# A fifth expert buffer made out of the dense weight buffers, in a two-layer attention and mixture-of-experts kernel on one core

## The reference

```python
for l in range(DEPTH):                       # DEPTH = 2
    sh1, sc1, g1, sh2, sc2, g2 = adaln_params(cond, w_ada[l], b_ada[l])
    ... = mixer_inputs(modulate(x, sh1, sc1), w_in[l], ...)     # two token mixers
    y = merge_branches(o_na, o_mla, gate_na, gate_mla, *out_w)
    x = layer_norm(DEEPNORM_ALPHA * x + g1 * y, ln1_g[l], ln1_b[l])
    y = hierarchical_moe(modulate(x, sh2, sc2), *moe_w)
    x = layer_norm(DEEPNORM_ALPHA * x + g2 * y, ln2_g[l], ln2_b[l])

def hierarchical_moe(h, ...):                # 32 experts, each token goes to 2
    ...
    hid = silu(einsum('bsd,edf->bsef', h, w_gate)) * einsum('bsd,edf->bsef', h, w_up)
    hid = hid * combine[..., None]
    return einsum('bsef,efd->bsd', hid, w_down)
```

## Time and profile before

| What | Value |
|---|---|
| median of 3 runs | 1138.49 us |
| the profiled execution | 1141.46 us |
| its span in the profile | 1139.3 us |
| TensorE busy | 971.6 us (85%) |
| VectorE, ScalarE busy | 318.4 us, 188.4 us |
| read from HBM | 329.38 MB |
| layer 0: first expert matmul, last scatter ends | 350.9 us, 578.0 us |
| layer 1: the same | 893.3 us, 1121.0 us |

### The profile page before, as it was taken

How to read it: one execution, slowest core, us unless ns; L and a number is a source line. 1 busy time by engine, 2 the same in 40 slices (tenths; PEclk the granted TensorE clock), 3 DMA queues, 4 the chain that set the end, 5 groups by cost and what they waited for, 6 DMA issues and landing times.

```text
span 1139.3 us, 15627 instructions
## 1 busy us (share of the span) xinstructions
PE 971.6 (85%) x6804; PEld 597.2 (52%) x6804; DVE 318.4 (28%) x630; ACT 188.4 (17%) x387; POOL 0.2 (0%) x4
## 2 busy tenths in 40 slices
PE   4399999989848998989829999998984899898993
PEld 1288767777644434333217786677874543433331
DVE  1203322222372212111171142232237221211215
ACT  0001311400012211111110122150001121111111
POOL 0000000000000000000000000000000000000000
PEclk7599999999958999999968999999995899999997
DMA  9656544477884999999954674446594499999990
GB/s 359 230 221 242 210 156 186 151 291 270 359 360 168 428 429 428 429 428 427 427 175 152 246 254 146 175 159 229 199 392 205 158 430 427 427 429 429 429 393 39
DMA packets 43227, 332.98 MB, mean 292 GB/s; under 512 B 5528, under 2 KB 7928, under 8 KB 13968
## 3 DMA queue, kind: packets, MB, share of 16 engines
q1 hardware_dynamic: 33552, 308.82, 67.0%
q10 hardware_dynamic: 9600, 23.07, 6.1%
HBM read 329.38 MB, written 2.49 MB: 291 GB/s over the span
## 4 chain that ended last, share of the span: by engine, by line
PE 73%; DMA 14%; DVE 7%; issue 3%; ACT 1%; SPq 0%; ACTq 0%; DVEq 0%
PE ps L671 15%; PE ps L487 10%; PE ps L684 8%; DMA expert_gate_up<-in_w_gu 7%; PE ps L511 5%; PE ps L602 5%; PE ps L612 4%; PE ps L423 4%; DMA expert_down<-in_w_dn 3%; PE ps L649 3%; PE ps L536 3%; PE ps L437 3%; PE ps L523 2%; PE ps L694 2%; PE ps L568 2%
## 5 line engine op out<-in xcount | busy, mean ns | idle before, releaser
L671 PE MATMUL ps<-expert_gate_up,gatheredT 128*32 128x512 f32 x2048 | 229.1, 600 | 16.6 <-DMA expert_gate_up<-in_w_gu 16.0
L671 PEld LDWEIGHTS ps<-expert_gate_up,gatheredT 128*32 128x32 f32 x2048 | 71.0, 111 | 164.3 <-issue 164.3
L684 PE MATMUL ps<-expert_down,hiddenT 128*32 128x512 f32 x1024 | 115.2, 595 | 9.3 <-issue 5.0
L487 PE MATMUL ps<-hT,dense 128*128 128x256 f32 x512 | 114.2, 381 | 0.0
L487 PEld LDWEIGHTS ps<-hT,dense 128*128 128x128 f32 x512 | 96.1, 190 | 16.0 <-issue 3.6
L1308 DVE TENSOR_TENSOR hidden<-hidden,ps 128x256 f32<-128x256 f32 x32 | 13.5, 421 | 234.0 <-ACT hidden L929 234.0
L684 PEld LDWEIGHTS ps<-expert_down,hiddenT 128*32 128x32 f32 x1024 | 32.2, 109 | 80.2 <-issue 50.6
L1318 DVE SCALAR_TENSOR_TENSOR y_lo<-ps,slot_weight,y_hi 128x512 fp32r<-128x512 f32 x64 | 48.0, 750 | 93.2 <-ACT y_hi L941 93.2
L437 PE MATMUL ps<-const,h_tokens 128*128 128x128 f32 x64 | 15.0, 426 | 68.0 <-DVE h_tokens L1024 68.0
L423 PE MATMUL ps<-dense,cond 128*32 128x256 f32 x768 | 57.2, 421 | 16.2 <-ACT cond L807 9.5
L511 PE MATMUL ps<-hT,dense 128*128 128x256 f32 x256 | 61.1, 399 | 2.2 <-DVE hT L975 2.2
(11 more groups left out here) (190 smaller groups left out, 963.2 us busy)
## 6 DMA issues: line engine op xcount, KB each, us to landing
expert_gate_up<-in_w_gu SPq DMA_DIRECT2D x64, 2048.0 KB, 17.4
expert_down<-in_w_dn SPq DMA_DIRECT2D x64, 1024.0 KB, 14.1
dense<-in_w_ada SPq DMA_DIRECT2D x48, 1024.0 KB, 5.0
dense<-in_w_in SPq DMA_DIRECT2D x28, 1024.0 KB, 6.6
dense<-in_w_o SPq DMA_DIRECT2D x8, 1024.0 KB, 6.3
dense<-in_w_out SPq DMA_DIRECT2D x8, 1024.0 KB, 6.9
shift<-ada_rows ACTq DMA_DIRECT2D x4, 1024.0 KB, 12.3
scale<-ada_rows ACTq DMA_DIRECT2D x4, 1024.0 KB, 8.5
```

What stands on the lines that cost most here:

```text
L487: last = mm(b[:, m * 256:(m + 1) * 256], w[:, k, m * P:(m + 1) * P], hT[:, k, :], start=(k == 0), stop=(k == KD - 1))
L671: last = mm(ps[r:r + 32, q, :], xgT[:, k, s, at_:at_ + CAP], w_gu[2 * q + j][:, k, :], start=(k == 0), stop=(k == KD - 1), skip_group_chec ...
L684: last = mm(ps[32 * e:32 * e + 32, 2 + c, :], hidT[:, e // 2, f, at_:at_ + CAP], w_dn[e][:, f, c * 512:(c + 1) * 512], start=(f == 0), sto ...
```

## The change

The expert part gets a fifth buffer (`SLOTS = 5`). It lies where the three dense buffers lie (3 x 8 KB = 24 KB): its gate and up half is on dense buffers 0 and 1, its down half on dense buffer 2. Expert e of a layer goes to buffer e mod 5 instead of e mod 4. The loop of SP over iterations is written out, and every load waits only for the last use of its own buffer (`gate_up_free`, `down_free`). The order on SP's queue stays: four gate-and-up loads, then four down loads. As the fifth buffer shares memory with the dense buffers, two waits are new: the gate-and-up load of expert 4 waits for TensorE's last use of the last three dense pieces, and the first dense load of layer 1 waits for `experts_done`, which VectorE counts up with the multiplication by `g2` (L1343 before). TensorE, VectorE and ScalarE do the same work in the same order; TensorE takes its weights from other buffer numbers and waits for the count of that buffer (`landed`).

```diff
+SLOTS = 5
-        w_gu = [at(f"expert_gate_up{j}", e_base + j * 24 * KB, [P, KD, 2 * FF]) for j in range(EPI)]
-        w_dn = [at(f"expert_down{j}", e_base + j * 24 * KB + 16 * KB, [P, 2, D]) for j in range(EPI)]
+        w_gu = [at(f"expert_gate_up{j}", e_base + j * 24 * KB, [P, KD, 2 * FF]) for j in range(SLOTS)]
+        w_dn = [at(f"expert_down{j}", e_base + j * 24 * KB + 16 * KB, [P, 2, D]) for j in range(SLOTS)]
+        def landed(r, e):
+            uses = len(range(e % SLOTS, NE, SLOTS))
+            return r * (16 * uses) + 16 * (e // SLOTS + 1)
+        def gate_up_free(r, e):
+            if e < SLOTS:
+                r, e = r - 1, max(range(e, NE, SLOTS))
+            else:
+                e = e - SLOTS
+            return r * (2 * ITERS) + e // 2 + 1
+        def down_free(r, e):
+            if e < SLOTS:
+                r, e = r - 1, max(range(e, NE, SLOTS))
+            else:
+                e = e - SLOTS
+            return r * (4 * ITERS) + 4 * (e // EPI) + 4
...
-            def expert_load(l, g, i, first):
+            def expert_loads(l, r):
                 m = M[l]
-                for q in range(2):
-                    if not first:
-                        sp.wait_ge(m["h_filled"], 2 * g + q - 1)
-                    for j in (2 * q, 2 * q + 1):
-                        src = io["w_gu"][l, ds(i * EPI + j, 1)].rearrange("o p k f -> (o p) k f")
-                        sp.dma_start(w_gu[j][:, :, :], src).then_inc(m["gu_in"][j], 16)
-                if not first:
-                    sp.wait_ge(m["y_filled"], 4 * g)
-                for j in range(EPI):
-                    src = io["w_dn"][l, ds(i * EPI + j, 1)].rearrange("o p k f -> (o p) k f")
-                    sp.dma_start(w_dn[j][:, :, :], src).then_inc(m["dn_in"][j], 16)
+                fresh = isinstance(r, int)
+                for e0 in range(0, NE, EPI):
+                    for e in range(e0, e0 + EPI):
+                        if not fresh or e >= SLOTS:
+                            sp.wait_ge(m["h_filled"], gate_up_free(r, e))
+                        elif e == SLOTS - 1:
+                            for n in range(slot_at[(l, "out", 3)] - DENSE_RING + 1, slot_at[(l, "out", 3)] + 1):
+                                sp.wait_ge(*last_use(n))
+                        sp.dma_start(w_gu[e % SLOTS][:, :, :], io["w_gu"][l, e]).then_inc(m["gu_in"][e % SLOTS], 16)
+                    for e in range(e0, e0 + EPI):
+                        if not fresh or e >= SLOTS:
+                            sp.wait_ge(m["y_filled"], down_free(r, e))
+                        sp.dma_start(w_dn[e % SLOTS][:, :, :], io["w_dn"][l, e]).then_inc(m["dn_in"][e % SLOTS], 16)
...
-                expert_load(l, 0, 0, True)
-                with sp.Fori(1, ITERS) as i:
-                    expert_load(l, i, i, False)
+                expert_loads(l, 0)
...
+                if l + 1 < DEPTH:
+                    sp.wait_ge(experts_done, l + 1)
...
-                link(V.tensor_tensor(y_acc[:, :, :], ps[:, 4:8, :].rearrange("p (s c) n -> p s (c n)", s=2), g2[:, :, :],
-                                     ALU.mult))
+                V.tensor_tensor(y_acc[:, :, :], ps[:, 4:8, :].rearrange("p (s c) n -> p s (c n)", s=2), g2[:, :, :],
+                                ALU.mult).then_inc(experts_done, 1)
+                dve.wait_ge(experts_done, l + 1)
```

More of the change, by code:

```diff
@@ L282, in build @@
             sem("member_ready"), sem("combine_ready"), sem("rounds_ready"), sem("hi_ready"), sem("lo_ready"))
-        dve_step, layer_done = sem("dve_step"), sem("layer_done")
+        dve_step, experts_done, layer_done = sem("dve_step"), sem("experts_done"), sem("layer_done")
         M = []
@@ L289, in build @@
                 "round_ready")})
-            M[l]["gu_in"] = [sem(f"gate_up_in{j}_{l}") for j in range(EPI)]
-            M[l]["dn_in"] = [sem(f"down_in{j}_{l}") for j in range(EPI)]
+            M[l]["gu_in"] = [sem(f"gate_up_in{j}_{l}") for j in range(SLOTS)]
+            M[l]["dn_in"] = [sem(f"down_in{j}_{l}") for j in range(SLOTS)]
         def nth(l, u):
@@ L376, in _ @@
                     with sp.Fori(1, r_end) as r:
-                        with sp.Fori(0, ITERS) as i:
-                            expert_load(l, r * ITERS + i, i, False)
+                        expert_loads(l, r)
+                if l + 1 < DEPTH:
+                    sp.wait_ge(experts_done, l + 1)
             sp.wait_ge(layer_done, DEPTH)
@@ L660, in select_T, with gate_up @@
                     last.then_inc(m["selT_filled"], 1)
-                def gate_up(g, i, q):
+                def gate_up(rd, i, q):
                     for j in range(2):
-                        pe.wait_ge(m["gu_in"][2 * q + j], g * 16 + 16)
+                        e = i * EPI + 2 * q + j
+                        pe.wait_ge(m["gu_in"][e % SLOTS], landed(rd, e))
                     for k in range(KD):
@@ L671, in gate_up, with down @@
                                 last = mm(ps[r:r + 32, q, :], xgT[:, k, s, at_:at_ + CAP],
-                                          w_gu[2 * q + j][:, k, :], start=(k == 0), stop=(k == KD - 1),
+                                          w_gu[(i * EPI + 2 * q + j) % SLOTS][:, k, :], start=(k == 0), stop=(k == KD - 1),
                                           skip_group_check=True)
                     last.then_inc(m["h_filled"], 1)
-                def down(g, s):
+                def down(g, i, s):
                     for c in range(2):
@@ L684, in down @@
                                 last = mm(ps[32 * e:32 * e + 32, 2 + c, :], hidT[:, e // 2, f, at_:at_ + CAP],
-                                          w_dn[e][:, f, c * 512:(c + 1) * 512], start=(f == 0), stop=(f == 1),
+                                          w_dn[(i * EPI + e) % SLOTS][:, f, c * 512:(c + 1) * 512], start=(f == 0), stop=(f == 1),
                                           skip_group_check=True)
@@ L711, in moe_round @@
                                 pe.wait_ge(m["selT_copied"], g + 1)
-                            gate_up(g, i, q)
+                            gate_up(r, i, q)
                             if i:
@@ L727, in moe_round @@
                             pe.wait_ge(m["xg_dve"], 4 * (n0 + (i + 1) // 2) + 4)
-                        for j in range(EPI):
-                            pe.wait_ge(m["dn_in"][j], g * 16 + 16)
+                        for e in range(i * EPI, i * EPI + EPI):
+                            pe.wait_ge(m["dn_in"][e % SLOTS], landed(r, e))
                         pe.wait_ge(m["hidT_copied"], g + 1)
                         for s in range(2):
-                            down(g, s)
+                            down(g, i, s)
                     for s in range(2):
```

## The result

The changed kernel takes 1128.33 us (median of 4 runs, 1125.36 to 1131.61) against 1138.14 us before. The ratio is 0.9903, 95% interval [0.9878, 0.9928]: about 11 us by the ratio, 9.8 us by the medians. So the three comparisons put the gain at 7.6 to 11.0 us; their mean, 0.9922, is 8.9 us. Predicted had been 8.2 us. The ratio of the first comparison, applied to the median of before (1138.49), gives 1127.4, just under the lower edge of the predicted range, 1128.0. The median itself lies just inside it.

A forecast was written before the change was run, and what follows sets the result against it. The prediction took the expert part to be limited by DMA bytes from 358 us on. Per layer, -4.9 us of early load and +0.8 us of stall gave -8.2 us over two layers: 1138.5 - 8.2 = 1130.3 us, range 1128.0 to 1135.0.

The forecast's parts named there:

- early load: Expert 4's gate-and-up load moves into the empty DMA stretch behind 342, taking 2.10 MB out of the limited stretch: -4.9 us per layer.
- stall of the queue: The DMA queue runs dry once per layer, at the down loads of experts 9 to 11: 0.8 us, bounds 0 to 1.6.
- expert parts, both layers: Early load and stall together over two layers: 2 x (-4.9 + 0.8) = -8.2 us.
- weaker waits, fifth buffer alone: Loads in the expert part may go earlier, but a queue already full delivers no faster: 0 us.
- wait between the layers: Layer 1's three dense loads go behind L1343, covered by VectorE's chain of 15.7 us: cost 0.
- all outside the expert parts: Rest of the kernel: no gain or loss; the profiled execution's 3.0 us above the median carried over.
- floor of TensorE: In the expert part, without the DMA, TensorE would need only some 10.5 us less per layer.
- Rival B: Queue runs dry more than once per layer in the expert part, one more stall of 1.6 us: 1135.1 us; chance 0.14.
- C: TensorE freed entirely in the expert part, five buffers taking all 10.5 us per layer away: 1117.5 us; chance 0.04.
- D: No change: early load collides with `g2`'s read or freed time is lost between matmuls; within 2.3 us of 1138.5; chance 0.06.
- E: Slower: dense loads or reads beside them arrive late between the layers, delaying layer 1 by 12 us: 1142.3 us; chance 0.06.
- rival A: The expert parts as worked out, with a stall of 0 to 1.6 us per layer: 1128.7 to 1131.9 us; chance 0.70.

The follow-up runs named there:

- x8: The changed kernel with SP's order shifted by one expert, 2 MB early as before and the original groups at the end; one execution, 1127.96 us, no ratio.
- x2: The changed kernel, but the gate-and-up load of expert 4 waits for h_filled = 1, so nothing is loaded early; ratio 1.0010.
- x3: The kernel before with four buffers, but layer 1's first three dense loads wait for the multiplication by g2; ratio 1.0003.
- x9: The changed kernel, but layer 1's first dense loads wait for the end of layer 0's last normalisation; ratio 0.9949.
- x7: The kernel before without the down loads of experts 4 to 31 of each layer, `down` using the first four experts' weights; ratio 0.9823.
- x5: The changed kernel with SP's order shifted by one expert, 3 MB per layer early and the original groups at the end; ratio 0.9887, 1123.68 us.
- x6: The changed kernel with the down load of expert 4 also early, the rest of SP's order as it was; ratio 0.9936.
- x11: The changed kernel, unaltered, timed a third time against the kernel before; ratio 0.9930.

## Where the prediction was right, and which step of it failed

| Step | Predicted | Measured |
|---|---|---|
| early load, per layer | -4.9 us | -5.2 and -5.1 us (x8, no stall, one trace) |
| stall of the queue, per layer | +0.8 us | +0.9 and +0.5 us (change against x8) |
| expert parts, both layers | -8.2 us | -8.9 us (two traces of before, three of the change) |
| weaker waits, fifth buffer alone | 0 | 0 (x2) |
| wait between the layers | 0 | 0 (x3, x9) |
| all outside the expert parts | 0 | -2.1 us by the first ratio, 0 by the mean of three |
| floor of TensorE, per layer | -10.5 us | -10.6 and -10.8 us (x7) |

**The limit and the mechanism** were right. Expert parts of before average 228.73 and 228.68 us over two traces, of the change 224.40 and 224.14 over three: 4.33 + 4.54 = 8.9 us. The last `down` starts 558.26 - 344.78 = 213.5 us after the first expert matmul, where 564.4 - 350.9 = 213.5 was forecast. Three doses bear it out: 0, 2 and 3 MB early (x2, x8, x5) give 0, 5.1 and 7.4 us per layer when the order never starves the queue, 2.5 us for each MB of 2^20 bytes, against 2.45 by the rate.

**The stall** came at the place and nearly with the size that was counted. The dip in the DMA share alone would have undersold it: 0.11 x 2 us of share is missing in 400:402. The GB/s beside it tell more: from 398 to 406 the four rows lack (18 + 104 + 14 + 6) x 2 = 284 KB against 428 GB/s, which is 0.7 us. The two other traces of the change have the same dip, 295 and 311 GB/s in their lowest 2 us. That it is a stall and can be had back by order is shown by x8, in one trace. The Trainium skill (DMA: Bandwidth & Descriptors, "Specifications") gives about 0.6 us to the first byte. Taken as the start of the full rate, as the prediction did, it would leave no stall, and there is one. But the 1.6 us of rows 2 and rows 4 are no first byte: they are the delay of a stream that is thought at full rate from its start, and this is what the count needs.

**Between the layers** nothing is lost, by x3 directly, and by x9 even 10.5 us later. In the change the three dense loads land 9 to 13 us after their issue, and the read of `sh1` beside them takes 11.4 instead of 9.3 us, so the two queues do share the engines. The rule of the Trainium skill (the same page, "Queues, rings and completion order") that each engine takes turns between its queues agrees with that.

**Rival B** (running dry more than once) did not happen in the change, but x6 shows that it was near: with 1 MB less of stock both dips came, and 3.9 to 4.4 us of 7.3 stayed. C fell by x7 and by the chain: the change's expert parts stay 6 us above TensorE's floor, and the bytes stay the limit. D and E fell by the times.

**The step that failed is the one from the expert parts to the whole kernel**, in the sum and in the range. The sum carried the profiled execution over (1138.5 - 8.2 = 1130.3) and so put everything outside the two expert parts at 0. The range gave that part no width either: its lower edge, 1128.0, lies 0.7 us under rival A's case without a stall, though the prediction itself said that a measurement can't tell 2.3 us from no change. The first ratio gives 11.0 us. Of these 8.9 us are the expert parts, 0.7 us more than the sum; the other 2.1 us lie outside them. Together they are the 2.8 us by which 1127.4 lies under the forecast, and the range had room for 2.3. In the two repeats the ratio gives 1.3 and 0.9 us less than the expert parts, and the mean of the three ratios is 8.9 us, the expert parts and nothing else. With 8.9 us the time would be 1129.6, well within the range. So what the runs show in place of the 0 is scatter between comparisons of one to two microseconds. That the first one was scatter is likely and not shown, as only one of its executions was profiled.

Where such scatter arises can be seen. The change's own runs spread by 6 us in the first comparison (1125.36 to 1131.61) and by 10 us in x11. The 16.1 us between the two profiled spans are 8.9 us of expert parts, 6.2 us ahead of layer 0's first expert matmul and 1.1 us in between. The 6.2 us lie in instructions that the change does not touch. Two pairs of rows show part of them; here is the change,

```profile
51.70 7.15 PE ps L534 x32
...
324.15 4.70 PE ps L649 x32
```

and here the same work in the kernel before.

```profile
53.32 9.35 PE ps L511 x32
...
327.57 7.03 PE ps L626 x32
```

The same 32 matmuls take 7.15 or 9.35 us, and 4.70 or 7.03 us, depending on the clock that TensorE is granted. In 51:61 it averaged 0.66 in the profile of before and 1.00 in that of the change. For the second pair it was 0.50 in 327.5:334.7 before and 0.77 in 324:329 with the change. Here 1.00 is 2.4 GHz and 0.50 is 1.2 GHz. These two pairs are 4.5 of the 6.2 us. Most of the rest, 1.6 us, has arisen ahead of the first pair; why is open. Over all thirteen traces of this study the first expert matmul starts anywhere from 344.8 to 350.9 us: on average at 348.0 in the five without an early load and at 347.4 in the eight with one. The 0.9903 of the first four runs is the largest gain of three comparisons. Whether the change favours the fast clock a little in the dense part is not excluded by this, as the 0.6 us between the two averages is far under the spread; no run shows it.

## What to carry to other kernels

In this stage, limited by bytes, a further buffer and weaker waits inside it gained nothing; only bytes moved out of it did, and each MB was worth its time at the full rate, up to the floor that the engine itself sets (10.6 us here). Taking them out also takes stock off the queue, so count, wait by wait, how long the queue lasts at each load that waits for late work, and put free loads ahead of it. At the end of the stage, look at what the engine still has to do after each of the last loads, and order the last groups by that: in this kernel order alone was worth some 3 us per layer with the same bytes early. And give the range of a forecast room for what differs between executions outside the stage: here 2.1 us of it, on top of 0.7 us that the sum was short, put the first measurement outside it.

## What the runs showed of the hardware

- The DMA stream from HBM to SBUF held 427 to 430 GB/s in stretches of 30 us through the expert part, on one core. Behind an issue to an idle queue it came as if at full rate from 1.6 us on (358.23 and 359.86); behind a full queue no such delay shows in the rate.
- Two queues share the DMA engines: the read of `sh1` took 9.3 us alone and 11.4 us beside three dense loads.
- The same 32 matmuls took 7.15 us with a granted clock of 1.00 and 9.35 us where the clock averaged 0.66 in the 10 us around them. Executions of one kernel spread by up to 0.9% (1125.36 to 1135.7); the expert parts, limited by the DMA, repeat within 0.4 us for one kernel, over two traces of before and three of the change.
